# Early up tiles of a PEER layer: high weights against high and low activations in one 512-column matmul

## The chip, the cores and the metric

The kernel runs on one core of a Trainium2 chip. The metric is the device time of one execution in microseconds (us); the median of 3 runs of the kernel before is 2183.82 us (2183.8 to 2184.14).

## The reference, cut to what matters

Two layers (`DEPTH = 2`) of a trunk with 256 tokens and 1024 channels. The change touches the second half of each layer, PEER: every token picks 16 of 128x128 = 16384 single-neuron experts in each of 8 heads.

```python
def peer_ffn(h, w_query, q_norm_peer, sub_keys_1, sub_keys_2, expert_u, expert_v):
    qr = rms_norm((h @ w_query).reshape(...), q_norm_peer)
    s1, s2 = ...                      # scores of the two halves of the key
    v1, i1 = lax.top_k(s1, 16); v2, i2 = lax.top_k(s2, 16)
    top_s, top_pos = lax.top_k(cand_s, 16)
    idx = jnp.take_along_axis(cand_i, top_pos, axis=-1)
    g = jax.nn.softmax(top_s, axis=-1)
    ...
    u = jnp.take(expert_u, ix, axis=0)
    act = jax.nn.gelu(jnp.einsum('td,ted->te', hx, u))
    vv = jnp.take(expert_v, ix, axis=0)
    return jnp.einsum('te,ted->td', (gx * act), vv)
```

## The kernel before, in words

The kernel does not gather experts. It computes `gelu(u_e . h)` for all 16384 experts and all tokens, multiplies by a gate that is zero where an expert was not picked, and multiplies by all of `expert_v`. All dense weights come as one stream of tiles of 128x1024 floats (512 KB each), 340 tiles a layer, in four raw buffers.

Each float is split in two: `hi` is the value rounded to the format that TensorE multiplies at one column per cycle (fp32r in the program), `lo` is the rest. For every weight tile ScalarE makes `hi` (`head`, L496), VectorE makes `lo = raw - hi` (`rest_of`, L873), both into four buffers. The activations `h` are split likewise, into `mov_hi` and `mov_lo`. TensorE then multiplies three of the four pairs (`product`, L1453 to L1455): `w_hi.m_hi + w_hi.m_lo + w_lo.m_hi`, all into the same 256 columns of PSUM.

A layer's PEER part has 256 tiles. The first 96 (`EARLY`) are the *early up tiles*: tile t holds the `u` of experts t*128 to t*128+127, as 8 chunks of 128 channels. TensorE does 8 x 3 matmuls of 256 columns (`project`, L1494) into one of two PSUM buffers `pj`, and ScalarE takes the result out with a gelu (`early_group`, L752, its activation at L757) into group t of the big buffer `arena`. Two buffers mean that TensorE can begin tile t+2 only when group t has been taken out (semaphore `out_free`). ScalarE's order for one tile is: `head` of tile t+3 (waits until tile t-1 is multiplied), then the taking out of tile t. So TensorE's tile t+3 depends on a chain that starts when tile t-1 ends: ScalarE `head`, VectorE `rest_of`.

Beside the early tiles VectorE works through the routing in a fixed written order (`split_early(n)` places the `rest_of` of the next n tiles between its steps): 17 rounds of top-k (L1264 to L1300), then four rounds that turn positions into indices (the loop at L1312, called *pick rounds* here: L1315 and L1321 on 128x2048 floats, L1326 a reduction over them), then a softmax that needs ScalarE in the middle (L767 to L775, two table loads), after 80 tiles (`EXP_AT`). The indices are turned by TensorE before tile 84 (`ROUTE_AT`) and copied at L1343.

Then come 32 *mix steps*: tile 96+n and, ahead of each half of it, four small matmuls (`tokens`, L1814) of one-hot matrices that make the gates of 8 tokens. The one-hots of the even quads are made by GpSimd (L484, four instructions a quad), those of the odd quads by ScalarE (L788, L792), `onehot_a` by VectorE (L1351). GpSimd begins them as soon as the indices are there. In the layer's first part GpSimd does two squarings (L458) and 16 scalings (L467). After the mix the 128 *down tiles* multiply with 512 columns (`down`).

The order on every engine is written out by hand; no scheduler moves anything.

Of the kernel before, what the change touches and what calls it, by code (L numbers as in the profile page):

```python
# [19 lines left out]
DEPTH, SEQ, D = 2, 256, 1024  # L20
P = 128
# [90 lines left out]
def trunk(nc, stream, par_dram, const_dram, mix_dram, taba_dram, keys_dram, front_dram, ada_dram, x_dram, out_dram):  # L112
# [4 lines left out]
    with ctx:  # L117
# [8 lines left out]
        hi = [sb(f"hi{i}", [P, 1024], f32r) for i in range(SPLIT)]  # L126
        lo = [sb(f"lo{i}", [P, 1024], f32r) for i in range(SPLIT)]
        x = sb("x", [P, KC, SEQ])
        mov_hi = sb("mov_hi", [P, 12, SEQ], f32r)
        mov_lo = sb("mov_lo", [P, 12, SEQ], f32r)  # L130
        w_hi = mov_hi[:, KC:KC + 4, :]
        w_lo = mov_lo[:, KC:KC + 4, :]
# [10 lines left out]
        gateT = sb("gateT", [P, SEQ])  # L143
        onehot_a = sb("onehot_a", [P, 8, NKEYS])

        onehot_b = [w.rearrange("p a b -> p (a b)").rearrange("p (r i) -> p r i", r=8) for w in (w_hi, w_lo)]

        ident = const[:, C_ID:C_ID + P]
        ones = const[:, C_ONE:C_ONE + P]
# [180 lines left out]
        route_ready = sem("route_ready")  # L330
        route_tr = sem("route_tr")
        route_in = sem("route_in")
        hot_a = sem("hot_a")
        hot_b = [sem("hot_b_even"), sem("hot_b_odd")]
        hot_used = sem("hot_used")
# [112 lines left out]
        @block.gpsimd  # L448
        def _(pool):
            for l in range(DEPTH):  # L450

                wait_alone(pool, sq_ready, 2 * KC * l + KC)
                nc.gpsimd.memset(f_rows.bitcast(f32), 0.0).then_inc(f_zero, 1)

                def squared(n, t0):

                    wait_alone(pool, out_free, l * OUTS + (t0 + 4 + 2))
                    nc.gpsimd.tensor_tensor(merged[:, 4 * n:4 * n + 4, :], projT[:, t0:t0 + 4, :], projT[:, t0:t0 + 4, :],  # L458
                                            ALU.mult).then_inc(qk_sq2, 1)
# [30 lines left out]
        def _(act):  # L490
# [45 lines left out]
            for l in range(DEPTH):  # L536
# [212 lines left out]
                    .then_inc(q_sum, 1)  # L749

                nc.scalar.preload_act_table(ACT.Gelu_apprx_tanh)
                def early_group(i, j, ahead=True):  # L752
                    t = L0 + i * 4 + (T_PEER + j)
                    if ahead:
                        head(t + AHEAD, j + AHEAD)
                    act.wait_ge(tile_done, t + 1 + SPLIT)
                    nc.scalar.activation(arena[:, bass.ds(i * 4 + j, 1), :].squeeze(1), pj[(j + 1) % 2][:, 0:SEQ],  # L757
                                         ACT.Gelu_apprx_tanh).then_inc(out_free, 1)


                for j in range(4):
                    early_group(l * 0, j, j >= 1)
# [98 lines left out]
        def _(dve):  # L861
# [80 lines left out]
            for l in range(DEPTH):  # L942
# [507 lines left out]
        def _(pe):  # L1450
# [28 lines left out]
            for l in range(DEPTH):  # L1479
# [293 lines left out]
                def turn_sums():  # L1773

                    pe.wait_ge(q_sum, l + 1)
                    for c in range(4):
                        pe.transpose(wk[:, 4, c * P:(c + 1) * P], q_square[:, c // 2, c % 2 * P:(c % 2 + 1) * P],
                                     ident).then_inc(q_turned, 1)

                def early_tile(j, between=None):  # L1780

                    project(L0 + (T_PEER + j), j, O_PEER + j, (j + 1) % 2, None if j else M_2, between=between,
                            between_at=KC - 1).then_inc(tile_done, 1)

                early_tile(0, last_scores)
                early_tile(1)
# [1 line left out]
                early_tile(3)  # L1788
                with pe.Fori(1, ROUTE_AT // 4) as i:
                    for j in range(4):  # L1790
                        project(L0 + i * 4 + (T_PEER + j), j, i * 4 + (O_PEER + j), (j + 1) % 2).then_inc(tile_done, 1)

                pe.wait_ge(route_ready, l + 1)
                pe.wait_ge(s_copied, 8 * l + 8)
# [2 lines left out]
                    for b in range(2):  # L1797
                        pe.transpose(wk[:, 2 * n + b, 0:P], src[:, b * P:(b + 1) * P], ident).then_inc(route_tr, 1)
                for j in range(EARLY - ROUTE_AT):
                    project(L0 + (T_PEER + ROUTE_AT + j), j, O_PEER + ROUTE_AT + j, (j + 1) % 2).then_inc(tile_done, 1)  # L1800

                wait_alone(pe, route_in, 6 * l + 6)
                def tokens(i, j, half):
# [174 lines left out]
```

## Time and profile before

| | |
|---|---|
| median of 3 runs | 2183.82 us |
| span of the profiled execution, first to last instruction | 2181.1 us |
| what lies around the span, against the median | 2.7 us |
| PE busy / VectorE busy / ScalarE busy / GpSimd busy | 2151.9 / 1680.4 / 1233.9 / 245.7 us |
| early up tiles of the first layer, about | 327 to 603 us |
| 32 mix steps of the first layer, about | 603 to 751 us |

The own device time of the profiled execution is not among the figures shown; its span is 2181.1 us. In the profile PE is TensorE's matmuls, PEld its weight loads, DVE is VectorE, ACT ScalarE, POOL GpSimd, SP the engine that issues the transfers. A matmul's listed duration (0.28 us) is longer than the distance from its start to the next start (0.12 us), since matmuls are pipelined; what a matmul costs is the distance. `x3` at a row of a timeline means three instructions merged into one row, in brackets stands how long the engine had been idle before and what ended that.

### The profile page before, as it was taken

Reading aid. Unit: us, or ns where it says so; the run is one execution under the profiler, and the core shown is the slowest. Engines: PE = TensorE matmul, PEld = TensorE weight load, DVE = VectorE, ACT = ScalarE, POOL = GpSimd, SP = SyncE. Lnnn points to the kernel's source line nnn. Section 1 sums busy time; section 2 is a strip of 40 time slices with the busy share of each in tenths; the row PEclk is TensorE's granted clock in tenths of the full one; section 3 lists DMA queues with packets and bytes.
Section 4 is the critical chain, followed back from the end, with each engine's and each line's share of the span. In section 5 each row is a group of like instructions: output and inputs, shape, how many; then the busy total and the mean of one; then the engine's idle time right before and its main releaser. Section 6 shows DMA issues by size and latency. Waiting matters only on the chain.

```text
span 2181.1 us, 43026 instructions
## 1 busy us (share of the span) xinstructions
PE 2151.9 (99%) x15008; PEld 1989.8 (91%) x15008; DVE 1680.4 (77%) x3258; ACT 1233.9 (57%) x2168; POOL 245.7 (11%) x298
## 2 busy tenths in 40 slices
PE   6999999999999999999999999999999999999999
PEld 5889999999999988888888899999999999888887
DVE  8777777889499956777577878788886997567765
ACT  5656575444577655555566565644455776555554
POOL 0210000000166400000002100000002662000000
PEclk8999999999999999999999999999999999999999
DMA  9466655555533367787665666455555334687864
GB/s 352 156 223 229 204 188 173 182 182 182 184 122 110 125 193 260 258 253 231 192 202 176 221 231 206 162 183 183 179 177 175 115 116 144 200 272 258 254 211 171
DMA packets 115440, 427.29 MB, mean 196 GB/s; under 512 B 12816, under 2 KB 13072, under 8 KB 113680
## 3 DMA queue, kind: packets, MB, share of 16 engines
q1 hardware_dynamic: 115344, 426.08, 58.2%
q8 instruction: 51, 0.84, 0.2%
q14 instruction: 45, 0.37, 0.0%
HBM read 424.99 MB, written 1.05 MB: 195 GB/s over the span
## 4 chain that ended last, share of the span: by engine, by line
PE 96%; DVE 2%; ACT 1%; DMA 1%; issue 0%; SPq 0%; ACTq 0%; DVEq 0%
PE pj L1453 18%; PE pj L1455 18%; PE pj L1454 18%; PE wk L1453 11%; PE wk L1455 11%; PE wk L1454 11%; PE wk L1814 5%; PE wk L1583 1%; PE wk L1560 1%; DMA arena<-in_front 1%; PE wk L1576 1%; PE wk L1522 1%; DVE arena L878 0%; PE wk L1743 0%; ACT hi L496 0%
## 5 line engine op out<-in xcount | busy, mean ns | idle before, releaser
L873 DVE TENSOR_TENSOR lo<-raw,hi 128x1024 fp32r<-128x1024 f32 x683 | 843.3, 1236 | 417.7 <-ACT hi L496 412.1
L496 ACT ACTIVATE hi<-raw 128x1024 fp32r<-128x1024 f32 x683 | 721.4, 1057 | 470.9 <-PE wk L1455 341.5
L1453 PE MATMUL pj<-mov_hi,hi 128*128 128x256 f32 x3008 | 867.8, 288 | 1.8 <-DVE x L1204 1.3
L1455 PE MATMUL pj<-mov_hi,lo 128*128 128x256 f32 x3008 | 851.5, 283 | 0.0
L1454 PE MATMUL pj<-mov_lo,hi 128*128 128x256 f32 x3008 | 850.9, 283 | 0.0
L1453 PEld LDWEIGHTS pj<-mov_hi,hi 128*128 128x128 f32 x3008 | 577.0, 192 | 10.9 <-issue 8.3
L1454 PEld LDWEIGHTS pj<-mov_lo,hi 128*128 128x128 f32 x3008 | 576.5, 192 | 0.1
L1455 PEld LDWEIGHTS pj<-mov_hi,lo 128*128 128x128 f32 x3008 | 575.9, 191 | 0.0
L1453 PE MATMUL wk<-hi,mov_hi 128*128 128x512 f32 x1024 | 398.5, 389 | 0.0
L1454 PE MATMUL wk<-lo,mov_hi 128*128 128x512 f32 x1024 | 398.4, 389 | 0.0
L1455 PE MATMUL wk<-hi,mov_lo 128*128 128x512 f32 x1024 | 398.4, 389 | 0.0
L484 POOL TENSOR_SCALAR mov_hi<-const,routes 128x128 fp32r<-128x128 f32 x256 | 199.4, 795 | 1012.8 <-DVE gateT L1343 866.7
L757 ACT ACTIVATE arena<-pj 128x256 f32 (+1 forms) x192 | 73.9, 385 | 275.4 <-PE pj L1455 275.4
L1455 PEld LDWEIGHTS wk<-hi,mov_lo 128*128 128x128 f32 x1024 | 192.2, 188 | 40.1
L1454 PEld LDWEIGHTS wk<-lo,mov_hi 128*128 128x128 f32 x1024 | 192.2, 188 | 39.9
L1453 PEld LDWEIGHTS wk<-hi,mov_hi 128*128 128x128 f32 x1024 | 192.2, 188 | 39.6
L1351 DVE TENSOR_SCALAR onehot_a<-const,routes,gateT 128x128 f32<-128x128 f32 x512 | 148.4, 352 | 2.2 <-PE wk L1814 2.2
L878 DVE SCALAR_TENSOR_TENSOR arena<-arena,silu_c 128x1024 f32<-128x1024 f32 x87 | 105.9, 1225 | 11.4 <-DMA arena<-in_ada 11.0
L1395 DVE TENSOR_TENSOR mov_lo<-arena,mov_hi 128x256 fp32r<-128x256 f32 x256 | 106.9, 418 | 0.0
L827 ACT ACTIVATE mov_hi<-arena 128x256 fp32r (+1 forms) x256 | 101.8, 399 | 2.8 <-DVE arena L1360 2.8
L788 ACT ACTIVATE mov_lo<-const,routes 128x128 fp32r<-128x128 f32 x256 | 81.0, 397 | 0.0
L1453 PE MATMUL pj<-u,hi 128*128 128x258 f32 x240 | 70.3, 293 | 3.2 <-DVE u L905 2.0
(207 smaller groups left out, 1896.1 us busy)
## 6 DMA issues: line engine op xcount, KB each, us to landing
raw<-in_stream SPq DMA_DIRECT2D x684, 512.0 KB, 3.4
arena<-in_ada SPq DMA_DIRECT2D x72, 512.0 KB, 4.8
onehot_a<-in_ada SPq DMA_DIRECT2D x24, 512.0 KB, 4.3
arena<-in_front SPq DMA_DIRECT2D x8, 1024.0 KB, 14.8
arena<-in_taba SPq DMA_DIRECT2D x2, 1536.0 KB, 8.7
arena<-in_keys SPq DMA_DIRECT2D x2, 1024.0 KB, 5.5
x<-in_xT SPq DMA_DIRECT2D x1, 1024.0 KB, 14.8
arena<-in_mix SPq DMA_DIRECT2D x2, 512.0 KB, 4.2
```

The costliest lines, as they stand in the source:

```text
L484: e = nc.gpsimd.tensor_scalar(onehot_b[0][:, quad % 4 * 2 + r, :], iota, idx2T[:, t:t + 1], None, ALU.is_equal)
L496: nc.scalar.activation(hi[j % SPLIT][:, :], raw[j % RAW][:, :], ACT.Copy).then_inc(hi_done, 1)
L788: e = nc.scalar.activation(onehot_b[1][:, slot + r, :], iota, ACT.Abs, bias=idx2T[:, quad * 4 + r:quad * 4 + r + 1], scale=-1.0)
L827: nc.scalar.activation(w_hi[:, s, :], group_of(n), ACT.Copy).then_inc(w_head, 1)
L873: nc.vector.tensor_tensor(lo[j % SPLIT][:, :], raw[j % RAW][:, :], hi[j % SPLIT][:, :].bitcast(f32), ALU.subtract).then_inc(lo_done, 1)
L878: nc.vector.scalar_tensor_tensor(tile, tile, 1.0, silu_c[:, :], ALU.mult, ALU.mult, accum_out=col)\
L1351: e = nc.vector.tensor_scalar(onehot_a[:, quad % 2 * 4 + r, :], iota, idx1T[:, t:t + 1], gateT[:, t:t + 1], ALU.is_equal, ALU.mult)
L1395: nc.vector.tensor_tensor(w_lo[:, s, :], group_of(n), w_hi[:, s, :].bitcast(f32), ALU.subtract).then_inc(w_rest, 1)
L1453: pe.matmul(out, w_h, m_h, start=first, stop=False)
L1454: pe.matmul(out, w_h, m_l, start=False, stop=False)
L1455: return pe.matmul(out, w_l, m_h, start=False, stop=last)
L1814: last = pe.matmul(wk[:, 2 + quad % 4, :].rearrange("p (i t) -> p t i", t=4)[:, r, :], onehot_a[:, quad % 2 * 4 + r, :], onehot_b[half][:, ...
```

## The change

The moving activations become one buffer in which chunk k's high and low halves lie side by side, so that 512 columns are high and low of one chunk. In the early up tiles TensorE multiplies `w_hi` with both halves at once (columns 0 to 255 of `pj` get the high product, 256 to 511 the low one) and `w_lo` with the high half alone: 16 matmuls a tile in place of 24. ScalarE copies both halves of `pj` to groups t and t+1 of `arena`, GpSimd adds group t+1 onto group t, and ScalarE does the gelu of group t in place, one tile later. Group t+1 is then overwritten by the next copy, so the copy of tile t+1 waits for the sum of tile t (`half_sum`).

```diff
-        mov_hi = sb("mov_hi", [P, 12, SEQ], f32r)
-        mov_lo = sb("mov_lo", [P, 12, SEQ], f32r)
+        mov = sb("mov", [P, KC + 4, 2, SEQ], f32r)
+        mov_hi, mov_lo = mov[:, :, 0, :], mov[:, :, 1, :]
...
 (GpSimd, ahead of its one-hots)
+                with pool.Fori(0, EARLY // 4) as i:
+                    for j in range(4):
+                        wait_alone(pool, out_free, i * 4 + (l * OUTS + O_PEER + j + 1 + 2))
+                        group = group_of(i * 4 + j)
+                        nc.gpsimd.tensor_tensor(group, group, group_of(i * 4 + (j + 1)), ALU.add).then_inc(half_sum, 1)

                 wait_alone(pool, route_in, 6 * l + 6)
...
 (ScalarE)
+                def early_gelu(i, j):
+                    group = group_of(i * 4 + j)
+                    nc.scalar.activation(group, group, ACT.Gelu_apprx_tanh).then_inc(gelu_done, 1)
+
+                def early_group(i, j, first=False):
                     t = L0 + i * 4 + (T_PEER + j)
-                    if ahead:
+                    if not first:
                         head(t + AHEAD, j + AHEAD)
+                        act.wait_ge(half_sum, i * 4 + (l * EARLY + j))
                     act.wait_ge(tile_done, t + 1 + SPLIT)
-                    nc.scalar.activation(arena[:, bass.ds(i * 4 + j, 1), :].squeeze(1), pj[(j + 1) % 2][:, 0:SEQ],
-                                         ACT.Gelu_apprx_tanh).then_inc(out_free, 1)
+                    nc.scalar.activation(arena[:, bass.ds(i * 4 + j, 2), :], pj[(j + 1) % 2][:, :].rearrange("p (h s) -> p h s", h=2),
+                                         ACT.Copy).then_inc(out_free, 1)
+                    if not first:
+                        early_gelu(i, j - 1)
...
 (VectorE, start of the mix)
-                dve.wait_ge(out_free, l * OUTS + (O_PEER + EARLY + 2))
                 for n in range(STEPS):
+                    if n == 1:
+                        dve.wait_ge(gelu_done, (l + 1) * EARLY)
...
 (TensorE, called for all 96 early tiles in place of project)
+                def project_wide(t, j, o, chunks=None, between=None):
+                    out = pj[(j + 1) % 2]
...
+                    for k in range(KC):
...
+                        if k == KC - 1:
+                            pe.matmul(out[:, 0:SEQ], w_l, mov_hi[:, k, :], start=False, stop=False)
+                            last = pe.matmul(out[:, :], w_h, both, start=False, stop=True)
+                        else:
+                            pe.matmul(out[:, :], w_h, both, start=k == 0, stop=False)
+                            pe.matmul(out[:, 0:SEQ], w_l, mov_hi[:, k, :], start=False, stop=False)
```

How the change moves instructions is shown at three places. First TensorE, two chunks in the loop over the early tiles. Before (`hi` and `lo` are the weights' halves):

```order
L1453 MATMUL pj<-mov_hi,hi 128x256
L1454 MATMUL pj<-mov_lo,hi 128x256
L1455 MATMUL pj<-mov_hi,lo 128x256
L1453 MATMUL pj<-mov_hi,hi 128x256
L1454 MATMUL pj<-mov_lo,hi 128x256
L1455 MATMUL pj<-mov_hi,lo 128x256
```

and now:

```order
L1816 MATMUL pj<-mov,hi 128x512
L1817 MATMUL pj<-mov,lo 128x256
L1816 MATMUL pj<-mov,hi 128x512
L1817 MATMUL pj<-mov,lo 128x256
L1813 MATMUL pj<-mov,lo 128x256
L1814 MATMUL pj<-mov,hi 128x512
```

Two of the three matmuls of a chunk have become one of twice the columns; in the last chunk the two are exchanged.

Second GpSimd, between its last scaling of the attention part and its one-hots. Before:

```order
L467 TENSOR_TENSOR arena<-arena,small 128x2x256
L484 TENSOR_SCALAR mov_hi<-const,routes 128x128 [waits route_in]
L484 TENSOR_SCALAR mov_hi<-const,routes 128x128 x7
L484 TENSOR_SCALAR mov_hi<-const,routes 128x128 [waits hot_used]
```

and now (the loop of four additions runs 24 times):

```order
L469 TENSOR_TENSOR arena<-arena,small 128x2x256
L480 UNCONDITIONAL_BRANCH
L480 ISA
L484 ISA [waits out_free]
L484 REGISTER_ALU
L484 TENSOR_TENSOR arena<-arena 128x256
...
L480 COMPARE_AND_BRANCH
L492 ISA [waits route_in]
L492 TENSOR_SCALAR mov<-const,routes 128x128 x8
L492 TENSOR_SCALAR mov<-const,routes 128x128 [waits hot_used]
```

The one-hots for the first mix steps now stand behind all 96 additions, the last of which waits for the copy of tile 95.

Third ScalarE, tiles 1 and 2. Before:

```order
L496 ACTIVATE hi<-raw 128x1024 [waits tile_done,raw_loaded0]
L757 ACTIVATE arena<-pj 128x256 [waits tile_done]
L496 ACTIVATE hi<-raw 128x1024 [waits tile_done,raw_loaded1]
L757 ACTIVATE arena<-pj 128x256 [waits tile_done]
L496 ACTIVATE hi<-raw 128x1024 [waits tile_done,raw_loaded2]
```

and now:

```order
L504 ACTIVATE hi<-raw 128x1024 [waits tile_done,raw_loaded0]
L771 ACTIVATE arena<-pj 128x512 [waits tile_done,half_sum]
L763 ACTIVATE arena<-arena 128x256
L504 ACTIVATE hi<-raw 128x1024 [waits tile_done,raw_loaded1]
L771 ACTIVATE arena<-pj 128x512 [waits tile_done,half_sum]
L763 ACTIVATE arena<-arena 128x256
L504 ACTIVATE hi<-raw 128x1024 [waits tile_done,raw_loaded2]
```

A copy and a gelu stand between two heads where a gelu alone stood, and the copy has a second wait, for GpSimd.

## Rows read from the trace of the kernel before

**Rows 1.** The page, part 4: the chain that ended last, by engine.
```profile
PE 96%; DVE 2%; ACT 1%; DMA 1%; issue 0%; SPq 0%; ACTq 0%; DVEq 0%
```
**Rows 2.** Waits of PE over the span: waiting instruction, releaser, us, times, longest.
```profile
PE wk L1475 <- DMA arena<-in_front: 13.9, 1, 13.9
...
PE pj L1453 <- DVE u L905: 2.0, 1, 2.0
...
PE pj L1453 <- ACT arena L757: 0.5, 2, 0.3
```
**Rows 3.** Stretches, early and down tiles: PE, PEld, DVE, ACT, POOL busy (count), clock.
```profile
350.00:500.00 150.00, 150.00 (x1252) 150.00 (x1251) 128.72 (x414) 70.70 (x104) 0.00 (x0) 1.00 0.54 182
800.00:900.00 100.00, 100.00 (x443) 82.81 (x442) 65.12 (x89) 50.40 (x74) 0.00 (x0) 1.00 0.73 245
```
**Rows 4.** Groups, shapes apart, whole span: busy us, mean ns, idle before.
```profile
L496 ACT ACTIVATE hi<-raw 128x1024 fp32r<-128x1024 f32 x683 | 721.4, 1057 | 470.9 <-PE wk L1455 341.5 <-PE pj L1455 123.2 <-DMA raw<-in_stream 2.8
...
L757 ACT ACTIVATE arena<-pj 128x256 f32 x176 | 67.8, 385 | 259.3 <-PE pj L1455 259.3
...
L573 ACT ACTIVATE arena<-pj 128x512 f32<-128x512 f32 x4 | 2.4, 592 | 0.0
```
**Rows 5.** Lines L467 and L484 on POOL: ns min/median/max.
```profile
L467 POOL TENSOR_TENSOR arena<-arena,small x32: 607/1038/2022, 77.4 to 1207.8; 128x256 f32<-128x256 f32 x16, 128x512 f32<-128x512 f32 x16
...
L484 POOL TENSOR_SCALAR mov_hi<-const,routes x256: 595/602/1652, 569.3 to 1815.7; 128x128 fp32r<-128x128 f32 x128
```
**Rows 6.** Timeline of DVE and POOL, attention part: start us, us, instruction.
```profile
76.89 0.16 DVE L1027 TENSOR_TENSOR small<-small 128x4 f32<-128x4 f32 x1
77.18 1.20 DVE L873 TENSOR_TENSOR lo<-raw,hi 128x1024 fp32r<-128x1024 f32 x1
77.45 4.95 POOL L467 TENSOR_TENSOR arena<-arena,small 128x256 f32<-128x256 f32 x4 [4.68 <-DVE small L1028]
78.30 0.57 DVE L1027 TENSOR_TENSOR small<-small 128x4 f32<-128x4 f32 x1
```
**Rows 7.** Timeline of DVE in the pick rounds.
```profile
501.44 2.28 DVE L1315 TENSOR_TENSOR arena<-arena,const 128x2048 f32<-128x2048 f32 x1
...
522.84 2.29 DVE L1315 TENSOR_TENSOR arena<-arena,const 128x2048 f32<-128x2048 f32 x1
525.04 2.35 DVE L873 TENSOR_TENSOR lo<-raw,hi 128x1024 fp32r<-128x1024 f32 x2
...
534.11 2.28 DVE L1315 TENSOR_TENSOR arena<-arena,const 128x2048 f32<-128x2048 f32 x1
...
544.23 1.23 DVE L873 TENSOR_TENSOR lo<-raw,hi 128x1024 fp32r<-128x1024 f32 x1
```
**Rows 8.** Timeline of ACT in the last pick round.
```profile
541.35 0.39 ACT L757 ACTIVATE arena<-pj 128x256 f32 x1 [1.55 <-PE pj L1455]
541.63 1.05 ACT L496 ACTIVATE hi<-raw 128x1024 fp32r<-128x1024 f32 x1
```
**Rows 9.** Timeline of ACT and PE where the softmax's two table loads stand.
```profile
555.75 0.39 ACT L757 ACTIVATE arena<-pj 128x256 f32 x1 [1.55 <-PE pj L1455]
...
561.15 0.37 ACT L757 ACTIVATE arena<-pj 128x256 f32 x1
...
561.66 0.36 PE L1453 MATMUL pj<-mov_hi,hi 128*128 128x256 f32 x1 [0.30 <-ACT arena L757]
```
**Rows 10.** Timeline of POOL after the routes, its first eight one-hots.
```profile
569.31 6.43 POOL L484 TENSOR_SCALAR mov_hi<-const,routes 128x128 fp32r<-128x128 f32 x8 [433.02 <-DVE gateT L1343]
```
**Rows 11.** Timeline of ACT and PEld, last early tiles and first mix step.
```profile
597.43 1.27 ACT L788 ACTIVATE mov_lo<-const,routes 128x128 fp32r<-128x128 f32 x4
...
602.59 0.98 PEld L1814 LDWEIGHTS wk<-mov_hi,onehot_a 128*128 128x128 f32 x8
...
602.91 0.38 ACT L757 ACTIVATE arena<-pj 128x256 f32<-128x256 f32 x1 [1.38 <-PE pj L1455]
```
**Rows 12.** A stretch at the start; columns as in Rows 3.
```profile
22.00:28.00 6.00, 6.00 (x22) 5.55 (x23) 6.00 (x12) 3.68 (x12) 0.31 (x1) 0.50 1.01 421
```

More of the change, by code:

```diff
@@ L128, in trunk @@
         x = sb("x", [P, KC, SEQ])
-        mov_hi = sb("mov_hi", [P, 12, SEQ], f32r)
-        mov_lo = sb("mov_lo", [P, 12, SEQ], f32r)
-        w_hi = mov_hi[:, KC:KC + 4, :]
-        w_lo = mov_lo[:, KC:KC + 4, :]
+        mov = sb("mov", [P, KC + 4, 2, SEQ], f32r)
+        mov_hi, mov_lo = mov[:, :, 0, :], mov[:, :, 1, :]
+        w_hi, w_lo = mov_hi[:, KC:KC + 4, :], mov_lo[:, KC:KC + 4, :]
         const = sb("const", [P, NCONST])
@@ L144, in trunk @@
         onehot_a = sb("onehot_a", [P, 8, NKEYS])
-        onehot_b = [w.rearrange("p a b -> p (a b)").rearrange("p (r i) -> p r i", r=8) for w in (w_hi, w_lo)]
+        onehot_b = [mov[:, k:k + 2, :, :].rearrange("p a h b -> p (a h b)").rearrange("p (r i) -> p r i", r=8)
+                    for k in (KC, KC + 2)]
         ident = const[:, C_ID:C_ID + P]
@@ L332, in trunk @@
         route_in = sem("route_in")
+        half_sum = sem("half_sum")
+        gelu_done = sem("gelu_done")
         hot_a = sem("hot_a")
@@ L751, in _ @@
                 nc.scalar.preload_act_table(ACT.Gelu_apprx_tanh)
-                def early_group(i, j, ahead=True):
+                def early_gelu(i, j):
+                    group = group_of(i * 4 + j)
+                    nc.scalar.activation(group, group, ACT.Gelu_apprx_tanh).then_inc(gelu_done, 1)
+                def early_group(i, j, first=False):
                     t = L0 + i * 4 + (T_PEER + j)
-                    if ahead:
+                    if not first:
                         head(t + AHEAD, j + AHEAD)
+                        act.wait_ge(half_sum, i * 4 + (l * EARLY + j))
                     act.wait_ge(tile_done, t + 1 + SPLIT)
-                    nc.scalar.activation(arena[:, bass.ds(i * 4 + j, 1), :].squeeze(1), pj[(j + 1) % 2][:, 0:SEQ],
-                                         ACT.Gelu_apprx_tanh).then_inc(out_free, 1)
+                    nc.scalar.activation(arena[:, bass.ds(i * 4 + j, 2), :], pj[(j + 1) % 2][:, :].rearrange("p (h s) -> p h s", h=2),
+                                         ACT.Copy).then_inc(out_free, 1)
+                    if not first:
+                        early_gelu(i, j - 1)
                 for j in range(4):
-                    early_group(l * 0, j, j >= 1)
+                    early_group(l * 0, j, j == 0)
                 with act.Fori(1, EXP_AT // 4) as i:
@@ L818, in _ @@
                     head(L0 + (T_MIX + n + AHEAD), n + AHEAD)
+                    if n == 0:
+                        act.wait_ge(half_sum, (l + 1) * EARLY)
+                        early_gelu(l * 0, EARLY - 1)
                     if n:
@@ L1778, in turn_sums @@
                                      ident).then_inc(q_turned, 1)
+                def project_wide(t, j, o, chunks=None, between=None):
+                    out = pj[(j + 1) % 2]
+                    pe.wait_ge(lo_done, t + 1)
+                    pe.wait_ge(out_free, l * OUTS + o + 1)
+                    for k in range(KC):
+                        if chunks is not None:
+                            pe.wait_ge(mov_ready, l * M_READY + (chunks + k + 1))
+                        if between is not None and k == KC - 1:
+                            between()
+                        w_h, w_l = chunk(j, k)
+                        both = mov[:, k, :, :].rearrange("p h s -> p (h s)")
+                        if k == KC - 1:
[4 more added lines that the diff above has]
+                            pe.matmul(out[:, 0:SEQ], w_l, mov_hi[:, k, :], start=False, stop=False)
+                    last.then_inc(tile_done, 1)
                 def early_tile(j, between=None):
-                    project(L0 + (T_PEER + j), j, O_PEER + j, (j + 1) % 2, None if j else M_2, between=between,
-                            between_at=KC - 1).then_inc(tile_done, 1)
+                    project_wide(L0 + (T_PEER + j), j, O_PEER + j, None if j else M_2, between)
                 early_tile(0, last_scores)
@@ L1790, in _ @@
                     for j in range(4):
-                        project(L0 + i * 4 + (T_PEER + j), j, i * 4 + (O_PEER + j), (j + 1) % 2).then_inc(tile_done, 1)
+                        project_wide(L0 + i * 4 + (T_PEER + j), j, i * 4 + (O_PEER + j))
                 pe.wait_ge(route_ready, l + 1)
@@ L1799, in _ @@
                 for j in range(EARLY - ROUTE_AT):
-                    project(L0 + (T_PEER + ROUTE_AT + j), j, O_PEER + ROUTE_AT + j, (j + 1) % 2).then_inc(tile_done, 1)
+                    project_wide(L0 + (T_PEER + ROUTE_AT + j), j, O_PEER + ROUTE_AT + j)
                 wait_alone(pe, route_in, 6 * l + 6)
```

## The prediction, made before the changed kernel was run

> **What bounds the kernel now.** I read the chain that ended last first: 96% of it is TensorE [rows 1]. Then the waits of TensorE: the only ones in the early tiles are two on ScalarE's L757, 0.5 us in both layers [rows 2]. So in the 96 early tiles of a layer the kernel is as fast as TensorE issues matmuls, and a matmul saved there is time saved, unless something else becomes late. Third, the stretches: between 350 and 500 us TensorE is never idle, VectorE is busy 128.7 of 150 us (86%), ScalarE 70.7 (47%), GpSimd not at all [rows 3]. VectorE is the next in line, and in the pick rounds it has no gaps whatever [rows 7]. The reader is to see that the margin above TensorE is thin in two places and wide elsewhere, and that the change adds work to ScalarE and GpSimd.
>
> **TensorE's gain.** In the rows of the stretches 1252 matmuls of 256 columns touch 150 us; less two that stick out at the edges that is 0.120 us each. In the down tiles 443 matmuls of 512 columns, less two, in 100 us are 0.2267 us each [rows 3]. Twice the columns costs 0.107 us more, not 0.120: each matmul has 0.013 us that does not depend on its columns. A tile had 24 x 0.120 = 2.88 us. Now it has 8 x (0.2267 + 0.120) = 2.773 us. The gain is 0.107 us a tile, 96 tiles x 2 layers x 0.107 = **20.5 us**, the 8 fixed parts that are no longer there. No stretch of the trace alternates 512 and 256 columns; the bounds are that the long one costs two short ones (gain 0) and that the fixed part vanishes for all 8 short ones too (gain 41). I take 20.5, since both lengths show the same fixed part.
>
> The Trainium skill, "TensorE: Matmul & The Clock Gate", on matmul duration, gives columns / 2.4 + 2.5 ns for a matmul at full clock. By it a tile would go from 24 x 109 = 2.62 to 8 x (216 + 109) = 2.60 us, and the gain would be 24 x 2.5 less 16 x 2.5 = 0.02 us a tile, an estimate of 3.8 us in all. The trace disagrees with it by 11 ns a matmul, and the rows' 0.013 us decides.
>
> **Start of the mix: a new wait.** GpSimd's one-hots now stand behind all 96 additions, and the first matmuls of the mix need the first four. Before they followed the last early matmul without a gap, at 602.59 [rows 11]; the one-hots had been made by 576 [rows 10]. Now, counted from the start of the last early matmul: before, ScalarE took tile 95 out 0.32 us after it (602.91 against 602.59, [rows 11]); the longer matmul adds 0.11, so 0.43. ScalarE's four one-hots, which stand two tiles earlier (597.43), make it late for tile 94, but by 95 it has caught up. The copy has the shape of L573, 0.59 us [rows 4]. GpSimd starts 0.2 us later and has to let VectorE's last `rest_of` finish (some 0.25). The addition is of the size of L467's smaller form, 0.61 us undisturbed [rows 5], 0.57 from start to start. Four one-hots: eight took 6.43 us in rows 10, of which two were held up (the longest took 1.65 for 0.60 [rows 5]); undisturbed 0.58 each from start to start, so 3 x 0.58 + 0.60 = 2.33. Then 0.1 to TensorE, less the 0.12 at which the next matmul would have started anyhow: 0.43 + 0.59 + 0.2 + 0.25 + 0.57 + 2.33 + 0.1 - 0.12 = **4.35 us a layer, 8.7 in all**. Nothing covers it: VectorE's next instruction and ScalarE's next one-hots wait for the use of the first. GpSimd needs 2.3 us for the next quad and a mix step takes 4.6 (148 us for 32), so it is late once. Bounds: 4.0 (nothing held up) to 5.7 (a one-hot and the addition each held up by a whole VectorE instruction).
>
> **The softmax on ScalarE.** After 80 tiles ScalarE has two table loads and three small instructions between two takings out, and the second comes too late: it runs at 561.15, and TensorE waits for it [rows 9]. The first of them would have been followed by a matmul 0.12 us after the one at 561.09, it came at 561.66: 0.5 us lost. Now ScalarE reaches the table load later, relative to the tile's end, by 0.11 (the last matmul is longer), by 0.21 (0.59 for 0.385) and by the gelu of 0.385, 0.7 in all [rows 4]; the second copy itself takes 0.2 longer; and TensorE wants the buffer 2 x 0.107 earlier. That is **1.1 us more a layer, 2.2 in all**. Bounds: 0.7 to 1.6.
>
> **GpSimd against VectorE in the pick rounds.** GpSimd did nothing beside the early tiles. Now it has an addition in each, and the two engines hold each other up. The row: L1027, an instruction on 128x4 elements, took 0.16 us at 76.89 and 0.57 at 78.30, right behind a `rest_of`, while a GpSimd instruction of 128x256, issued at 77.45, was under way [rows 6]; GpSimd for its part took 1.4 us or more for such an instruction where 0.61 is the least [rows 5, 6]. So the GpSimd instruction waited for the `rest_of` to end, went first, and held VectorE's next one for 0.42 us.
>
> The Trainium skill, "SBUF — State Buffer", says that the pair of ports shared by VectorE and GpSimd is an exclusive lock, held for the whole instruction, and that a VectorE instruction with two inputs in SBUF contends with a GpSimd one that reads SBUF. By it a reduction is free of it and `rest_of`, L1315 and L1321 are not; the trace agrees in the 0.42 us of L1027, and has nothing on the reduction.
>
> In the top-k rounds this costs nothing, I think: the addition runs 1.3 to 1.9 us after the tile's end and the `rest_of` that tile's end releases starts 2.6 us after it, and VectorE has 14% of gaps. In the pick rounds VectorE has none: from 501.44 to 545.46 it does 15 `rest_of` and four rounds [rows 7], one round and four tiles in 534.11 - 522.84 = 11.27 us, where TensorE took 11.52 and will want 11.09. What is its reserve? The `rest_of` at 544.23 belongs to the `head` at 541.63 [rows 8]. ScalarE takes a tile out 0.42 us after the start of its last matmul in this loop, so that of the tile before was at 541.35 - 0.42 = 540.93; TensorE wants the new tile 3 tiles and 0.12 us later, at 549.69, and it is ready at 545.46: 4.2 us are in reserve. From this go 0.7 us by which ScalarE's chain is later, as at the softmax; 18 tiles x 0.107 = 1.9; and the additions: 15 of them, of which 3 fall under the reduction, one of a round's three long parts, so 12 x 0.42 = 5.0. 4.2 - 0.7 - 1.9 - 5.0 = **-3.4: TensorE waits 3.4 us a layer, 6.8 in all**. Bounds: if an addition costs VectorE nothing, 1.6 us of reserve are left and the wait is 0; if all 15 cost their full 0.61, 9.2 in place of 5.0, the wait is 7.6 a layer. I take the held 0.42, the only row that shows the two engines back to back.
>
> **What costs nothing.** ScalarE's sum per tile, 1.06 + 0.59 + 0.385 = 2.0 [rows 4], fits in 2.77. The copy's wait for `half_sum` is met 0.8 us after the copy before, up to 3 us if VectorE keeps GpSimd out through L1315, and is asked for 2.77 after it; TensorE has a second buffer on top. The gate on `gelu_done` is met while VectorE waits for its second one-hots. The side-by-side layout changes strides only. No transfer moves.
>
> **Sum.** -20.5 + 8.7 + 2.2 + 6.8 = -2.8. The span goes from 2181.1 to 2178.3, and with the 2.7 around it the time is **2181 us**. A measurement of this kernel tells about 0.2% (4.4 us) from no change, so this is no change.
>
> **Rivals.**
> A. *The additions slip in beside VectorE* (the hold of L1027 is the exception, or falls where VectorE has reserve). Then the 6.8 go, and the time is 2174.2. For it: the hold is read from one instruction of another shape. Against it: VectorE has no gaps in those 44 us.
> B. *The clock falls in the new wait.* TensorE is idle 4.35 us at the start of each mix. The granted clock is 1.0 in the stretches of rows 3, but at the start, after a wait of 13.9 us [rows 2] it stood at 0.50 while TensorE was busy from 22 to 28 [rows 12]; that is 1.2 GHz for 2.4. The longest other wait in what follows is 2.0 us [rows 2], so nothing shows what 4.35 do. If it falls and stays low for the same 6 us of work, 3 us are lost each time: 6 in all, 2187 us, slower than before. It decides from the point where the wait is longer than the clock tolerates; with one of the two hit it is 2184.
> The Trainium skill, "TensorE: Matmul & The Clock Gate", on re-throttling, warns against idle gaps between bursts of matmuls, since the clock falls in them. By it this rival would hold at both mixes, 2187 us.
> C. *The ring ScalarE, GpSimd, VectorE drags.* If VectorE's back-to-back instructions keep GpSimd out for more than one of theirs, the additions come late, the copies wait, and TensorE waits for both; or the top-k rounds lose reserve as well: 1.27 us of routing and 1.16 of `rest_of` a tile (86% of 2.88 is 2.48) plus 0.42 are 2.90, above 2.77, and 60 tiles x 0.13 are 8 us a layer, 16 in all: 2197. Against it: the phases, as told.
> D. *The 512-column matmul costs two short ones when the lengths alternate.* Then 20.5 go: 2201.5. Little speaks for it.
>
> **Chances.** The forecast 0.42; A 0.18; B 0.22; C 0.13; D 0.05. The forecast's own range, from the bounds of the three waits, is 2174 to 2192 if all went one way at once, and 2177 to 2186 if the largest alone goes half way. The range of 8 in 10 reaches to A's time and into C: 2173 to 2193. Faster by over 0.2% means below 2179.4: A, and a third of the forecast's case, 0.32. Slower means above 2188.2: D, C and a third of B, 0.25. Within: 0.43.
>
> **What would show it.** In the profile after: 2.77 us from tile to tile in 350 to 500 us; waits of TensorE on GpSimd at the start of each mix, 4 to 5 us, twice; waits on VectorE's `rest_of` of about 3.5 us a layer where the pick rounds stand, with `rest_of`, L1315 and L1321 longer than before; on ScalarE's copy about 1.6 in place of 0.5 us a layer at the softmax. I am wrong if there is no such wait on `rest_of` (A), if the granted clock is below 1 at the start of the mix (B), if TensorE waits in the top-k rounds (C), or if the tile stays at 2.88 (D).

## The result and the profile after

The changed kernel takes 2200.93 us (median of 4 runs, 2199.51 to 2201.52) against 2183.95 us of the kernel before: ratio 1.0077, 95% interval 1.0063 to 1.0092. It is slower by 17 us, where 2181 had been forecast; the time lies outside the range of 2173 to 2193. The profiled execution took 2201.29 us, its span is 2199.5 us, so 1.8 us lie around the span; the span is 18.4 us longer than the 2181.1 us of before.

The page of the changed kernel, busy time of each engine (share of the span, instructions) and the chain that ended last:

```profile
PE 2150.7 (98%) x13472; PEld 1914.1 (87%) x13472; DVE 1703.5 (77%) x3258; ACT 1329.6 (60%) x2360; POOL 409.5 (19%) x490
...
PE 90%; DVE 6%; issue 1%; ACT 1%; DMA 1%; POOL 0%; SPq 0%; ACTq 0%; POOLq 0%; DVEq 0%
```

TensorE's busy time fell by 1.2 us only, though 1536 matmuls are gone, and its share of the chain went from 96% [rows 1] to 90%. The waits of TensorE over the span that the change brought or lengthened (line, releaser, us in all, times, longest); of them [rows 2] has the one on ScalarE's taking out alone, at 0.5 us in all:

```profile
PE wk L1853 <- POOL mov L492: 8.5, 2, 4.3
...
PE pj L1816 <- DVE lo L892: 4.9, 9, 1.2
PE pj L1816 <- ACT arena L771: 3.8, 4, 1.1
PE wk L1596 <- issue: 2.2, 1, 2.2
```

In the changed kernel L1853 is the mix's token matmul, L492 the one-hots, L892 `rest_of`, L504 `head`, L771 the copy, L763 the gelu, L484 the addition, L1334, L1340 and L1345 the three long parts of a pick round, L1596 a transpose of the attention. These rows count from a matmul's modelled end; below, distances go from start to start. The first three are the three waits that were forecast. The fourth was not, and stands in the second layer's attention, where the change touches nothing.

**The tile.** The stretch that answers to the first row of [rows 3], with the same columns:

```profile
350.00:500.00 150.00, 150.00 (x853) 130.50 (x852) 134.20 (x418) 98.26 (x159) 39.80 (x53) 1.00 0.56 185
```

853 matmuls, less two at the edges, in 150 us are 0.1763 us, 16 of them 2.820 us. The forecast was 2.773, and the tile of before took 2.88. Inside a tile (timeline of PE: start us, us, instruction):

```profile
422.00 0.40 PE L1816 MATMUL pj<-mov,hi 128*128 128x512 f32 x1
422.24 0.28 PE L1817 MATMUL pj<-mov,lo 128*128 128x256 f32 x1
422.36 0.40 PE L1816 MATMUL pj<-mov,hi 128*128 128x512 f32 x1
422.60 0.28 PE L1817 MATMUL pj<-mov,lo 128*128 128x256 f32 x1
422.71 0.40 PE L1816 MATMUL pj<-mov,hi 128*128 128x512 f32 x1
```

The short matmul follows 0.24 us after the long one (0.236 over many), where long ones among themselves stand 0.2267 apart [rows 3], and the long one follows 0.117 after the short one: 0.3525 a pair, against a forecast of 0.3467.

**The pick rounds.** Timeline of DVE (answers to [rows 7]):

```profile
507.28 2.27 DVE L1345 TENSOR_REDUCE arena<-arena 128x128 f32<-128x2048 f32 x1
...
510.73 2.82 DVE L1334 TENSOR_TENSOR arena<-arena,const 128x2048 f32<-128x2048 f32 x1
...
516.29 2.82 DVE L1340 TENSOR_TENSOR arena<-arena 128x2048 f32<-128x2048 f32 x1
...
520.17 2.27 DVE L1345 TENSOR_REDUCE arena<-arena 128x128 f32<-128x2048 f32 x1
522.48 1.64 DVE L892 TENSOR_TENSOR lo<-raw,hi 128x1024 fp32r<-128x1024 f32 x1
524.04 2.28 DVE L1334 TENSOR_TENSOR arena<-arena,const 128x2048 f32<-128x2048 f32 x1
```

and of POOL beside it:

```profile
507.34 0.74 POOL L484 TENSOR_TENSOR arena<-arena  x1 [1.06 <-ACT arena L771]
509.63 1.78 POOL L484 TENSOR_TENSOR arena<-arena  x1 [1.55 <-ACT arena L771]
...
522.29 0.74 POOL L484 TENSOR_TENSOR arena<-arena  x1 [1.44 <-ACT arena L771]
```

The parts with two inputs take 2.28 us, or 2.82 where an addition pushes in ahead of them: 0.54 us more. `rest_of` goes from 1.22 to 1.76 in the same way. The addition takes 0.74 us alone and up to 2.38 when it waits for VectorE. The reduction L1345 stays at 2.27 us in all eight rounds, and the addition that runs wholly under it (507.34) takes 0.74: between these two kinds there is no hold. An addition that starts in the reduction's last 0.15 us (522.29) still holds the `rest_of` behind it, which takes 1.64 us, 0.42 more. Over the rounds VectorE's instructions are longer by 6.6 us in the first layer and 7.4 in the second.

TensorE stands still six times in each layer's rounds. In the first layer the six tiles with such a wait are longer than 2.82 us by 1.39, 0.42, 1.02, 0.42, 1.05 and 0.42, together 4.7 us; in the second it is 5.0, and there the profile puts two of the six (0.80 us each) down to ScalarE's copy and not to `rest_of`.

**The softmax.** TensorE's wait after ScalarE's two table loads (answers to [rows 9]), then ScalarE's rows:

```profile
562.26 0.47 PE L1816 MATMUL pj<-mov,hi 128*128 128x512 f32 x1 [1.14 <-ACT arena L771]
```

```profile
559.28 1.28 ACT L791 ACT_TABLE_LOAD   x1
560.58 1.06 ACT L504 ACTIVATE hi<-raw 128x1024 fp32r<-128x1024 f32 x1
561.54 0.58 ACT L771 ACTIVATE arena<-pj 128x512 f32 x1
```

The distance from the matmul before is 1.53 us. The tile with this wait takes 4.20 us, 1.38 more than the others; before it took 3.41, 0.53 more than the others. That is 0.85 more a layer.

**The start of the mix.** POOL, then PE, then two stretches (the column behind POOL's is the granted clock):

```profile
603.57 0.77 POOL L484 TENSOR_TENSOR arena<-arena  x1 [0.95 <-ACT arena L771]
604.40 8.00 POOL L492 TENSOR_SCALAR mov<-const,routes 128x128 fp32r<-128x128 f32 x12
```

```profile
602.22 0.39 PE L1814 MATMUL pj<-mov,hi 128*128 128x512 f32 x1
606.89 2.05 PE L1853 MATMUL wk<-mov,onehot_a 128*128 128x128 f32 x8 [4.29 <-POOL mov L492]
...
608.95 0.41 PE L1474 MATMUL pj<-mov,hi 128*128 128x256 f32 x1
609.16 0.41 PE L1475 MATMUL pj<-mov,lo 128*128 128x256 f32 x1
```

```profile
607.00:609.50 2.50, 2.50 (x12) 2.50 (x13) 0.52 (x2) 0.00 (x0) 2.42 (x5) 0.50 0.12 43
...
613.00:615.00 2.00, 2.00 (x19) 2.00 (x19) 1.86 (x5) 0.36 (x1) 0.00 (x0) 1.00 0.55 213
```

The wait is 4.67 us from start to start. Without one the next matmul starts 0.24 us after such a long one, so 4.44 us are lost here and 4.36 in the second layer. Behind the wait the granted clock is 0.50, that is 1.2 GHz: the matmuls of 256 columns stand 0.21 us apart instead of 0.12. It stays so for 6.8 us, at both mixes of this execution. TensorE does not wait again in the mix, yet from its first one-hot matmul to the start of its last half step it takes 149.41 us in the first layer and 149.20 in the second, where the kernel before takes 146.58: the low clock costs 2.8 and 2.6 us.

**The sum of the differences.** Tiles 192 x (2.820 - 2.880) = -11.5; pick rounds 9.7; softmax 1.7; mix waits 8.8; clock behind them 5.4; second attention 4.5; and -0.3 since the first tiles of a layer and those right behind a wait take 2.79 us and not 2.82. That makes 18.3, the span grew by 18.4.

### The profile page after: what moved, and what is told of

Its sections match the earlier page's. It is cut to its first block, busy times and chain, and to the rows that moved or that the text cites. A ratio compares the mean times of both kernels' runs of the same rounds, so it can differ in the third digit from the quotient of the medians.

```text
span 2199.5 us, 41274 instructions
## 1 busy us (share of the span) xinstructions
PE 2150.7 (98%) x13472; PEld 1914.1 (87%) x13472; DVE 1703.5 (77%) x3258; ACT 1329.6 (60%) x2360; POOL 409.5 (19%) x490
## 3 DMA queue, kind: packets, MB, share of 16 engines
HBM read 424.99 MB, written 1.05 MB: 194 GB/s over the span
## 4 chain that ended last, share of the span: by engine, by line
PE 90%; DVE 6%; issue 1%; ACT 1%; DMA 1%; POOL 0%; SPq 0%; ACTq 0%; POOLq 0%; DVEq 0%
PE pj L1816 11%; PE wk L1475 10%; PE wk L1473 10%; PE wk L1474 10%; PE pj L1473 10%; PE pj L1475 10%; PE pj L1474 10%; PE pj L1817 6%; PE wk L1853 5%; DVE lo L892 2%; PE pj L1814 2%; DVE arena L1340 1%; DVE arena L1334 1%; PE wk L1603 1%; DVE arena L1345 1%
## 5 line engine op out<-in xcount | busy, mean ns | idle before, releaser
L892 DVE TENSOR_TENSOR lo<-raw,hi 128x1024 fp32r<-128x1024 f32 x683 | 851.9, 1249 | 399.0 <-ACT hi L504 393.2
L504 ACT ACTIVATE hi<-raw 128x1024 fp32r<-128x1024 f32 x683 | 721.1, 1056 | 478.9 <-PE wk L1475 341.5
L1816 PE MATMUL pj<-mov,hi 128*128 128x512 f32 x1344 | 483.3, 398 | 8.8 <-DVE lo L892 4.9
L1473 PE MATMUL pj<-mov,hi 128*128 128x256 f32 x1472 | 434.3, 295 | 1.3 <-DVE x L1223 1.3
L1475 PE MATMUL pj<-mov,lo 128*128 128x256 f32 x1472 | 418.6, 284 | 0.0
L1474 PE MATMUL pj<-mov,hi 128*128 128x256 f32 x1472 | 418.0, 284 | 0.0
L1473 PE MATMUL wk<-hi,mov 128*128 128x512 f32 x1024 | 398.5, 389 | 0.0
L1475 PE MATMUL wk<-hi,mov 128*128 128x512 f32 x1024 | 398.4, 389 | 0.0
L1474 PE MATMUL wk<-lo,mov 128*128 128x512 f32 x1024 | 398.3, 389 | 0.0
L1817 PE MATMUL pj<-mov,lo 128*128 128x256 f32 x1344 | 377.0, 281 | 0.0
L484 POOL TENSOR_TENSOR arena<-arena x192 | 168.2, 876 | 770.5 <-ACT arena L771 770.5
L1816 PEld LDWEIGHTS pj<-mov,hi 128*128 128x128 f32 x1344 | 252.8, 188 | 65.5 <-ACT arena L771 5.1
L1473 PEld LDWEIGHTS pj<-mov,hi 128*128 128x128 f32 x1472 | 284.1, 193 | 9.2 <-issue 7.0
L1474 PEld LDWEIGHTS pj<-mov,hi 128*128 128x128 f32 x1472 | 283.5, 193 | 0.1
L1475 PEld LDWEIGHTS pj<-mov,lo 128*128 128x128 f32 x1472 | 282.9, 192 | 0.0
L1817 PEld LDWEIGHTS pj<-mov,lo 128*128 128x128 f32 x1344 | 253.9, 189 | 7.8
L1474 PEld LDWEIGHTS wk<-lo,mov 128*128 128x128 f32 x1024 | 192.2, 188 | 39.9
L1473 PEld LDWEIGHTS wk<-hi,mov 128*128 128x128 f32 x1024 | 192.2, 188 | 39.9
L1475 PEld LDWEIGHTS wk<-hi,mov 128*128 128x128 f32 x1024 | 192.2, 188 | 39.8
L771 ACT ACTIVATE arena<-pj 128x512 f32 (+1 forms) x192 | 114.9, 598 | 184.4 <-PE pj L1814 176.8
L492 POOL TENSOR_SCALAR mov<-const,routes 128x128 fp32r<-128x128 f32 x256 | 196.8, 785 | 92.7 <-PE wk L1853 92.5
```

The source lines that it names most:

```text
L484: nc.gpsimd.tensor_tensor(group, group, group_of(i * 4 + (j + 1)), ALU.add).then_inc(half_sum, 1)
L504: nc.scalar.activation(hi[j % SPLIT][:, :], raw[j % RAW][:, :], ACT.Copy).then_inc(hi_done, 1)
L771: nc.scalar.activation(arena[:, bass.ds(i * 4 + j, 2), :], pj[(j + 1) % 2][:, :].rearrange("p (h s) -> p h s", h=2), ACT.Copy).then_inc(ou ...
L892: nc.vector.tensor_tensor(lo[j % SPLIT][:, :], raw[j % RAW][:, :], hi[j % SPLIT][:, :].bitcast(f32), ALU.subtract).then_inc(lo_done, 1)
L1473: pe.matmul(out, w_h, m_h, start=first, stop=False)
L1474: pe.matmul(out, w_h, m_l, start=False, stop=False)
```

## The experiments

### The order of the widths

```diff
-for k in range(KC): wide(k), narrow(k)      (the last piece the other way round)
+for k in range(KC - 1): wide(k)
+between()
+for k in range(KC): narrow(k)
+wide(KC - 1)
```

> The changed kernel, but in each early tile seven 512-column matmuls stand first, then the eight of 256 columns, then the last of 512: two changes of length a tile in place of sixteen. Theory 1 (each change between the lengths costs some ns: in the changed kernel a pair takes 0.3525 us where 0.2267 + 0.120 were expected): the tile goes from 2.82 to 2.78 us, 7.5 us less in all, of which about 1 is given back in the pick rounds: 2194.5 us. Rival (the 512-column matmul is slower here whatever stands beside it, through what other engines read and write): the tile stays at 2.82, 2201 us.

Measured: 2195.0 us (2194.38 to 2198.8), ratio 1.0051 [1.0034, 1.0067]. The same stretch, and the tile (PE timeline; L1808 and L1816 are the long matmuls, L1815 the short ones):

```profile
350.00:500.00 150.00, 150.00 (x862) 132.05 (x861) 135.27 (x424) 99.43 (x162) 40.67 (x54) 1.00 0.54 185
```

```profile
420.61 1.12 PE L1815 MATMUL pj<-mov,lo 128*128 128x256 f32 x8
421.56 0.40 PE L1816 MATMUL pj<-mov,hi 128*128 128x512 f32 x1
421.80 1.32 PE L1808 MATMUL pj<-mov,hi 128*128 128x512 f32 x5
```

The tile takes 2.793 us, 0.027 less with the same 16 matmuls: the gain is 0.087 us a tile and not 0.060, where 0.107 had been forecast. The order thus accounts for 0.027 of the missing 0.047 us. It is not simply a price for each change of length. In this trace the one change from long to short costs nothing (0.2267 us from the long matmul to the short one behind it), but the long ones among themselves stand 0.230 apart (mean of 320 distances from 350 to 500 us), where those of the down tiles stand 0.2267 apart in the same run. So each of the two theories holds in part, and what makes a long matmul slower in these tiles is not shown.

### The first one-hots ahead of the last additions

```diff
+HOTS_AT = 88
 for each early group g:
     add(g)
+    if g == 88: wait(route_in); one_hots(quad 0)
+    if g == 90: one_hots(quad 2)
```

> The changed kernel, but GpSimd makes its first two quads of one-hots behind the additions of tiles 88 and 90 in place of behind tile 95's. Theory 1 (the wait at the start of the mix, 4.6 us a layer, comes from this order, and the fall of the granted clock behind it, 2.35 us a layer, from this wait): no wait of TensorE on GpSimd, no stretch of clock 0.5 at the mix, 9.1 + 4.7 us less: 2187 us. Rival (the clock falls for another reason): the wait goes, the clock falls all the same, 2192 us. Rival (VectorE, nearly full in the mix, takes over as bound): 2195 us or more.

Measured: 2187.68 us (2184.58 to 2187.79, 10 runs), ratio 1.0015 [1.0005, 1.0024]. The mix now starts without a gap, and the clock stays up there (PE timeline, and the same stretch as before):

```profile
603.07 0.40 PE L1827 MATMUL pj<-mov,hi 128*128 128x512 f32 x1
603.31 1.06 PE L1866 MATMUL wk<-mov,onehot_a 128*128 128x128 f32 x8
```

```profile
607.00:609.50 2.50, 2.50 (x24) 2.50 (x23) 2.50 (x7) 1.72 (x3) 1.67 (x3) 1.00 0.65 198
```

13.3 us come back, where wait and clock together are 8.8 + 5.4 = 14.2 in the changed kernel's trace. The largest loss was the place of eight instructions in GpSimd's program.

### No additions

```diff
-nc.gpsimd.tensor_tensor(group, group, next_group, ALU.add).then_inc(half_sum, 1)
+pool.sem_inc(half_sum, 1)
```

This leaves out the sum of the two halves; copies, gelus and waits stay.

> The changed kernel without GpSimd's addition: it only raises the semaphore, so the low product is left out of the result. Theory 1 (GpSimd's additions and VectorE's instructions shut each other out, and this makes TensorE wait 4.8 us a layer in the pick rounds): L1334, L1340 and rest_of return to 2.28 and 1.22 us, the waits on rest_of are gone, and the wait at the mix is 0.7 shorter a layer: 9.6 + 1.5 less, 2190 us. Rival (the later chain of ScalarE and the faster tile use up VectorE's reserve by themselves): half of the waits or more stay, 2195 us or more.

Measured: 2189.3 us (2188.47 to 2191.08, 7 runs), ratio 1.0027 [1.0016, 1.0039]. The waits of PE from 500 to 566 us, and DVE in the pick rounds:

```profile
PE pj L1815 <- ACT arena L770: 1.1, 1, 1.1
```

```profile
509.20 2.29 DVE L1333 TENSOR_TENSOR arena<-arena,const 128x2048 f32<-128x2048 f32 x1
511.40 2.35 DVE L891 TENSOR_TENSOR lo<-raw,hi 128x1024 fp32r<-128x1024 f32 x2
513.67 2.28 DVE L1339 TENSOR_TENSOR arena<-arena 128x2048 f32<-128x2048 f32 x1
```

No two-input part is above 2.29 us, and TensorE no longer waits in the rounds of either layer: the pick rounds' loss comes from GpSimd's additions, not from ScalarE being later, for its copies stay. The softmax's wait stays as well (1.53 us from start to start, behind the matmul at 556.72), so that one does not come from the additions. The mix wait is 4.15 us in place of 4.67.

### The kernel before, with the wait alone

```diff
 wait_alone(pool, route_in, 6 * l + 6)
+wait_alone(pool, out_free, l * OUTS + O_PEER + EARLY + 2)
 for quad in range(0, QUADS, 2): ...
```

Nothing else is changed: GpSimd's one-hots start when tile 95 has been taken out.

> The kernel before, with one wait more: GpSimd begins its one-hots only when tile 95 has been taken out. Nothing else is changed. TensorE has to wait 0.32 + 0.385 + 0.2 + 2.33 us, about 3.2, at the start of each mix. Theory 1 (such a wait makes the granted clock fall): 3.2 + 2.35 a layer, 2183.9 + 11.1 = 2195 us, with a stretch of clock 0.5 behind each mix's start. Rival (3.2 us are too short for that, or the clock's fall has another cause): 2190.3 us, clock 1.0 throughout.

Measured: 2194.39 us (2192.68 to 2195.17), ratio 1.005 [1.0033, 1.0067]; the profile is of the run of 2192.68. PE at the mix, and two stretches:

```profile
603.32 0.28 PE L1456 MATMUL pj<-mov_hi,lo 128*128 128x256 f32 x1
606.73 2.04 PE L1815 MATMUL wk<-mov_hi,onehot_a 128*128 128x128 f32 x8 [3.13 <-POOL mov_hi L485]
```

```profile
607.00:609.50 2.50, 2.50 (x13) 2.50 (x13) 0.61 (x3) 0.00 (x0) 2.42 (x5) 0.50 0.07 28
610.00:612.50 2.50, 2.50 (x24) 2.50 (x23) 2.05 (x5) 0.00 (x0) 2.25 (x3) 1.00 0.11 13
```

A wait of 3.41 us from start to start brings the clock down as well, here for 3.4 us. In the profiled run two waits (6.6 us) and two falls (3.0 us, from mixes of 148.07 and 148.13 us against 146.58) make 9.6 of the 9.8 us by which its span is longer. No wait was added but these two, and 10.5 us are lost by the medians: wait and clock at the mix are a cost of their own that needs no wide matmul.

### Both remedies

The early one-hots and the wide matmuls first, `between` moved behind the short ones.

> The changed kernel with the first eight one-hots placed between the additions (as in the run that did this alone, 2187.68 us) and, in each early tile, the eight weight pieces' 512-column matmuls (one kept for the end) before the eight of 256 columns. The theory that each change of width between two matmuls costs a few ns: the tile's pitch falls from 2.820 to 2.793 us, as it did with the same order alone, on the 76 tiles of a layer outside the pick rounds, 2 us a layer and 4 in all: 2183.7 us. What is left to explain against a gain of 0.087 us a tile would be the pick rounds (4.8 us a layer) and the second layer's attention (4.5 us). Rival, that the order's gain was only seen because PE was held up elsewhere: 2187 us or more.

Measured: 2182.79 us (2180.42 to 2183.91, 11 runs), ratio 0.9995 [0.9985, 1.0004]. What is left is no gain: the pick rounds, the softmax and part of the second attention's stall eat it. In the profile of this kernel, taken of its fastest run, that stall was 0.9 us; what it was in the other runs is not shown.

### The wide form for 56 tiles

```diff
+WIDE = 56
 early tiles 0 to 55:  eight wide matmuls, eight short ones, copy, addition, gelu
+early tiles 56 to 95: as in the kernel before, gelu straight out of PSUM, no addition
```

The wide tiles have the order of the previous experiment, and GpSimd's one-hots stand behind 56 additions only.

> The wide form, with the 512-column matmuls first, for early tiles 0 to 55 of each layer alone, tiles 56 to 95 as in the kernel before; GpSimd's one-hots, the pick rounds and the softmax then stand as before. The theory (the additions under the pick rounds, ScalarE's copies under the softmax and the addition ahead of the one-hots made all the loss outside the second layer's attention): 56 x 2 x 0.087 = 9.7 us less than the kernel before, some 0.5 us lost where the first tile starts: 2174.6 us if the second layer's attention runs as before, 2179 if its stall of 4.5 us is there. Rival, that the faster tiles only bring VectorE's pick rounds to the front and the time is given back there: 2183 us.

Measured: 2173.9 us (2173.24 to 2174.2, 5 runs), ratio 0.9954 [0.9941, 0.9968]. It beats both kernels, by 9.8 us and by 27. Its only wait of PE between 327 and 610 us, and its chain:

```profile
PE pj L1487 <- ACT arena L791: 0.3, 1, 0.3
```

```profile
PE 96%; DVE 2%; ACT 1%; DMA 1%; issue 0%; SPq 0%; ACTq 0%; DVEq 0%
```

The faster tiles bring TensorE earlier into the pick rounds, and nothing is given back there: VectorE's work comes forward with them. The rival falls. Order and number of wide tiles differ from the changed kernel at once; against the kernel with both remedies, which has the same order, the 40 tiles that went back to the old form bring 8.9 us.

### The fetch of TensorE's program

```diff
+if l == 0:
+    for _ in range(64): pe.sem_inc(padded, 1)
 wait_alone(pe, route_in, 6 * l + 6)      # TensorE, start of the mix
```

The stall in the second attention stands in the profiles of the kernels with wide tiles in all 96 places (the changed one and four experiments above; full in four of the five, 0.9 us in the last) and in no other. Its first sign is on VectorE, which waits for modulation weights. In the changed kernel SP issues them, VectorE gets them, and the list of transfers of the stretch 1197.0 to 1202.6 has:

```profile
1197.04 0.43 SPq L390 DMA_DIRECT2D arena<-in_ada  x1
```

```profile
1202.57 1.23 DVE L897 SCALAR_TENSOR_TENSOR arena<-arena,silu_c 128x1024 f32<-128x1024 f32 x1 [1.98 <-DMA arena<-in_ada]
```

```profile
q8 instruction: 1, 0.02, 1.0%
...
arena<-in_ada SPq DMA_DIRECT2D x1, 512.0 KB, 5.5
```

In the kernel before, where all of this stands 7.05 us earlier, the same transfer:

```profile
1189.97 0.43 SPq L388 DMA_DIRECT2D arena<-in_ada  x1
```

```profile
1194.12 1.23 DVE L878 SCALAR_TENSOR_TENSOR arena<-arena,silu_c 128x1024 f32<-128x1024 f32 x1 [0.59 <-DMA arena<-in_ada]
```

```profile
arena<-in_ada SPq DMA_DIRECT2D x1, 512.0 KB, 4.1
```

The transfer took 5.5 us instead of 4.1. A packet of 16 KB of program code (q8) was fetched meanwhile, 2.3 us after the transfer was issued; in the kernel before it comes 4.1 us earlier against the work, 1.8 us before the transfer is issued. In the kernel with both remedies the fetch comes 1.9 us behind the issue and the transfer takes 5.1 us: there the stall is 0.9 us. From VectorE's delay follows GpSimd's, and TensorE's 2.2 us at L1596, behind which the clock is granted at 0.5 for 3.4 us.

> The changed kernel with 64 semaphore increments more in TensorE's program, in the first layer just ahead of the wait in which TensorE stands idle for the one-hots, so that they cost nothing, or up to 1 us, there; no work is added or left out. Theory of the stall in the second layer's attention (4.5 us, in every kernel that has the changed tiles and in none without): TensorE's program is shorter by 160 matmuls and their weight loads a layer, 320 instructions, so a fetch of its code (16 KB in one packet) comes 4.1 us later against the work and falls into the load of the modulation weights, which lands late. 320 is one fetch of 256 and 64 more, if a matmul and its weight load are 64 bytes each; with 64 put back the fetch is where it was, 59.4 us behind the same point instead of 63.5, and the stall goes: 2196.5 us. Rival, that the stall is due to the tiles' layout or to ScalarE and VectorE, which the padding leaves alone: 2201 us.

Measured: 2198.96 us (2198.87 to 2199.61, 5 runs), ratio 1.007 [1.0056, 1.0084]; 2.0 us less than the changed kernel. The same three rows:

```profile
1199.05 0.43 SPq L392 DMA_DIRECT2D arena<-in_ada  x1
```

```profile
1203.24 1.23 DVE L899 SCALAR_TENSOR_TENSOR arena<-arena,silu_c 128x1024 f32<-128x1024 f32 x1 [0.64 <-DMA arena<-in_ada]
```

```profile
arena<-in_ada SPq DMA_DIRECT2D x1, 512.0 KB, 4.2
```

The fetch is back at 59.5 us behind the second layer's eleventh `rest_of` (before: 59.4; changed: 63.5), the transfer takes 4.2 us, TensorE does not wait at that transpose, and the second attention is 4.2 us shorter than in the changed kernel. The time fell by less than expected because the increments were not free: GpSimd's one-hots were there as before, but TensorE came to them only 7.76 us after its last early matmul instead of 4.67. That is 64 increments at 0.12 us, longer than the wait they were to hide in; at the end of the mix 2.1 us of it are still lost. The place of the fetch is thus shown to be the cause. That the two transfers meet on one of the 16 DMA engines is inferred from the durations, not shown.

## Why the prediction was wrong

Against the forecast span of 2178.3 us the measured one is 21.2 us longer; around the span lie 1.8 us and not 2.7. By the prediction's own steps:

- **TensorE's gain**: the failed term. 20.5 us were forecast, 11.5 came, 0.060 us a tile in place of 0.107. "Both lengths show the same fixed part" holds for rows of one length; the trace had no alternation, and there a pair takes 0.3525 us and not 0.2267 + 0.120. That is 9.0 us of the miss. With the long ones together the gain would be 0.087 a tile; why the rest is missing stays open. Rival D named the place, but at twice the price and more. That its 2201.5 us lie next to the measured time is chance: the tile did not stay at 2.88, and the rest came from waits and clock. The bounds of the gain (0 to 41) held it, but the range did not take them in.
- **Start of the mix**: mechanism and size right, 4.44 and 4.36 us against 4.35. The sum took off 0.12 us for the next matmul's start, where behind a long one it is 0.23, so its other terms were 0.1 to 0.2 too small together. 0.1 us.
- **Clock**: it stood in the forecast's sum at nothing, and this is the second step that failed. Rival B came true at both mixes, at 2.8 and 2.6 us instead of 3. The kernel before shows the same with the wait alone. The Trainium skill, "TensorE: Matmul & The Clock Gate", section "Why this matters for your kernels", asks for no idle gaps between bursts of matmuls, since the clock falls in them; the trace agrees, with the granted clock at 0.50 after waits of 4.67 and 3.41 us. I gave it 0.22 because "nothing shows what 4.35 do"; the only row at hand, the start, spoke for it. 5.4 us.
- **Pick rounds**: mechanism right, size off: 4.7 and 5.0 us against 3.4. I had taken 0.42 us for what an addition holds; it is 0.54 of a 0.74-us addition in most cases, and VectorE lost 6.6 and 7.4 us to it, not 5.0. Rival A, that the additions slip in, fell. What the Trainium skill, "SBUF — State Buffer", section "Who interferes with whom", says of the shared ports holds here: parts with two inputs lose 0.54 us, the reduction nothing. 2.9 us for both layers.
- **Softmax**: 0.85 against 1.1 a layer, inside its bounds. -0.5 us.
- **What costs nothing**: in the top-k rounds that is so: the tile stays at 2.82 us there, and rival C did not come. Its sum was too high by a slip as well: 1.27 + 1.16 + 0.42 are 2.85 us, not 2.90. "No transfer moves" was wrong. A shorter program moves the fetches of its own code, and one of them fell on a transfer with no reserve: 4.5 us in the second attention, in none of my cases.

9.0 + 0.1 + 5.4 + 2.9 - 0.5 + 4.5, and -0.3 for the quicker tiles, make 21.1 us. The result passed the range since four misses of one sign came together. Two were knowable: the gain had a lower bound of 0 that the range ignored, and the clock had a rule and a row.

## What to carry to other kernels

Put work that the next stage waits for ahead of the last piece of the stage before, also on an engine that is nearly idle: eight instructions behind a chain cost 13.3 us here, over a third of it through the clock. Use a cheaper form of a stage only where the engines behind it have room: the change on 56 of 96 tiles, in the grouped order, turned +17 us into -9.8. Group matmuls by width rather than alternating them, which was worth 0.027 us a tile here. And where a stall appears in a part that a change doesn't touch, look at the code fetches among the transfers before blaming chance.

## What was not expected of the hardware

- A matmul of 256 columns behind one of 512 starts 0.236 us after it, 512 behind 512 after 0.2267, and 512 behind 256 after 0.117 (256 behind 256: 0.120). A pair costs 5.8 ns more than its parts. Grouped, 512 behind 512 takes 0.230 in these tiles; the tile is 2.793 us grouped and 2.820 alternating.
- GpSimd's addition of two 128x256 tiles takes 0.74 us, and a VectorE instruction with two inputs that it gets ahead of is 0.54 us longer in most cases (0.33 to 0.49 right behind a reduction).
- The clock fell after distances of 4.67, 3.41 and, in the second attention, 2.47 us between two matmuls' starts, but not after 1.53, and not after one of 2.43 at 32.8 us in the kernel before or of 2.58 at 33.5 us in the one with 56 wide tiles; so the length of the gap alone does not settle it. In the second attention it fell 1.3 us after TensorE had started again. It stood at 0.50 for 3.4 or 6.8 us, not always the same at the same place.
- One fetch of 16 KB of code during a 512-KB transfer made that transfer 1.4 us longer, and a semaphore increment alone in TensorE's program takes 0.12 us.
